# A two-block transformer kernel on one core: forget sums, masks and the permuted modulation sums leave TensorE, and the last weight tile comes by pieces

## The chip, the core and the metric

The kernel runs on one core of a Trainium2 chip. The core has five engines with their own instruction streams: TensorE (PE, with its weight loads PEld), VectorE (DVE), ScalarE (ACT), GpSimd (POOL) and SyncE (SP), whose stream here only issues DMA. They hand work over by semaphores. The metric is the device time of one launch in microseconds, median of the runs.

## The reference

Two transformer blocks over one sequence of 256 tokens with 1024 channels, all in float32.

```python
# first block
mod = c @ w_ada + b_ada                      # shift, scale, gate
h = rmsnorm(x, norm_g) * (1 + scale) + shift
q_a, k_a, v_a, z_a, q_b, k_b, v_b, z_b, f_logit, g_logit = split(h @ w_in)
y_a = stick_breaking(q_a, k_a, v_a)          # w = exp(logsig(z) + sum over later s of logsig(-z)), s < t
y_a = (y_a * silu(z_a)) @ w_o_sb
F = cumsum(log_sigmoid(f_logit + b_forget), axis=1)
y_b = softmax(q_b.k_b / 8 + F[t] - F[s], s <= t) @ v_b      # forgetting attention, 8 heads
y_b = (y_b * silu(z_b)) @ w_o_fox
x = x + gate * ((sigmoid(g0) * y_a + sigmoid(g1) * y_b) @ w_out);  x = rmsnorm(x, final_g)
# second block
mod2 = silu(c_2) @ w_ada_2 + b_ada_2         # sh1, sc1, g1, sh2, sc2, g2
x = x + g1 * (mix(attention(h), conv(h)) @ w_out_2)
h2 = rms_norm(x, norm2_w) * (1 + sc2) + sh2
x = x + g2 * moe(h2)                         # 64 experts, top 1 of 8 groups, top 2 in it; w1, w3, w2
```

## The kernel before, in words

Every engine has one stream written out by hand; nothing is scheduled by a tool. 256 tokens are two tiles of 128 partitions, 1024 channels are eight chunks.

**Up to 290 us: the first block.** The weights come in chunks of 2 MB through a ring of four slots (`RING`, 16 KB per partition each). `proj(q)` is the number of the chunk with 512 columns of w_in, `mod2(q)` that of 512 columns of w_ada_2; they alternate, projection first. `read_by` says for each chunk who must have read it before its slot is filled again; SP issues them in order (L396 to L399). PE works through "units": half a chunk each, 16 matmuls of 256 columns (L618) or 8 of 512 (L629). A float32 matmul shows as two records in the trace. Unit u writes PSUM bank u % 2 and may start when unit u-2 has been taken out (`unit_free`). Chunks 0 to 11 are k, q, v, z of the stick-breaking attention (units 0 to 7), the same of the forgetting attention (8 to 15) and the gate logits (16 to 23). Between the halves of the units the stream places other work: in units 6 to 13 the stick-breaking attention of four head pairs m (`stick_scores`, `stick_after`, `stick_pv`), in units 14 to 22 the forgetting ("fox") attention (`fox_scores`, `fox_transposes`, `fox_pv`), after every odd unit from 5 `mod2_out`.

**mod2.** DVE multiplies a chunk of w_ada_2 by silu(c_2) per partition and adds its eight parts up (`mod2_part`, L1677 and L1679, one half of it per unit). `mod2_out` sums over the partitions on PE; for q = 6 to 9 it takes every eighth column, 8 matmuls, so that the result is laid out as the expert weights are (L653). All these small results go through bank 7, one after another (`misc_done`, `misc_free`).

**Masks and sums on PE.** `stick_after` adds the suffix sums to the scores in PSUM by three matmuls and then adds -1e30 above the diagonal by two more, identity times `never` (L693, L694). `fox_scores` adds -F[s] by three matmuls per head over tiles U that POOL makes from log f (L743 to L745 and L2249 to L2251). DVE's `row_max` then adds the mask, writes the row to SBUF and takes its maximum; ACT takes Exp, DVE the reciprocal, ACT scales, PE transposes.

**silu(z).** ACT writes exp(-z) of units 6, 7, 14, 15; DVE adds 1, takes the reciprocal (3.35 us for 512 columns) and multiplies by z, still in PSUM (L1737), which frees the bank. The gates of units 16 to 21 get the same sigmoid at u = 16 to 21 (`sigmoid_tail`).

**290 to 500 us: the second block's attention and router**, paced by PE again. POOL multiplies the router weights by the second block's scale (L2271 to L2275, after `ab2_ok`).

**From 500 us: the experts.** 16 rounds of four experts; w1, w3 and w2 of four experts are 8 MB each. SP fills eight slots in turn. In the last round w2 comes by quarters, j = 0 to 3, 16 DMAs of 512 KB. After the last quarter PE finishes both halves of the columns (L1167), DVE scales (L2151), PE combines (L1177), DVE adds (L2157), SP stores four pieces (L485).

**The start.** PE multiplies c by w_ada (L549) as four slices of 1 MB land, transposes x (L534), turns the sums into columns (L559) and starts the first halves of units 0 and 1 (L586). `keep_clock(n, bank)` (L525) issues n matmuls of 256 columns whose result nobody reads.

## Time and profile before

| | |
|---|---|
| median of 3 runs | 1414.81 us (1414.81 to 1416.65) |
| span of the profiled execution | 1409.6 us; its own time isn't listed apart from the runs', the median lies 5.2 us over the span |
| PE busy | 1013.6 us, 72% of the span |
| DVE, ACT, POOL busy | 454.7, 167.5, 59.2 us |
| moved by DMA | 503.77 MB, mean 357 GB/s |
| PE busy, 59.0 to 172.0 us | 111.91 of 113.00 us |
| DMA, 518.5 to 1397.7 us | 426 GB/s |
| chain that ended last | PE 50%, DMA 41%, DVE 3%, SP's issues 3% |

The page shows two programs one behind the other. Until about 500 us PE's digits are 9 and the DMA's 4 to 7; after it the DMA's are 9 throughout and PE's 3 to 6. Shares over the whole span say little on either. Two engines' records can overlap, and a matmul's end is modelled: where matmuls follow each other, the distance of two starts is the step, and the printed duration is up to 0.16 us more.

### The profile page before, as it was taken

To read this page: it belongs to the slowest core of one execution; us is meant where nothing else is said; L and a number is where in the kernel's file an instruction comes from. 1 tells how busy PE (TensorE), PEld (TensorE's weight loads), DVE (VectorE), ACT (ScalarE), POOL (GpSimd) and SP (SyncE) were. 2 spreads that over 40 slices of the span, in tenths; PEclk is the share of its full clock that TensorE was granted. 3 is DMA by queue.
4 is the path that set the end of the run, shared out by engine and by line. 5 is a ranking of instruction groups with operands and counts; after the bars stand their busy time and mean duration, and the time that the engine had idled before them with its cause. 6 is when DMAs were issued, how large, how long until landed. Compare 5 with 4: busy or idle time off the path is not lost.

```text
span 1409.6 us, 14940 instructions
## 1 busy us (share of the span) xinstructions
PE 1013.6 (72%) x6025; PEld 530.5 (38%) x6025; DVE 454.7 (32%) x932; ACT 167.5 (12%) x413; POOL 59.2 (4%) x94
## 2 busy tenths in 40 slices
PE   6999999999899985646656366563665646666366
PEld 4677688655456532212222122221222212122121
DVE  1465575542577542112121121211212112121121
ACT  1233232012333200000000000000000000000000
POOL 3101120011020000000000000000000000000000
PEclk9999999999999998868888787897878868788688
DMA  9976655675527899999999999999999999999996
GB/s 357 355 287 238 235 184 213 239 147 192 210 97 294 332 370 428 429 428 428 427 428 429 428 429 428 428 430 427 429 427 429 429 427 430 427 429 427 429 426 271
DMA packets 81551, 503.77 MB, mean 357 GB/s; under 512 B 5670, under 2 KB 11070, under 8 KB 57444
## 3 DMA queue, kind: packets, MB, share of 16 engines
q1 hardware_dynamic: 78784, 496.22, 86.3%
q0 software_dynamic: 2656, 6.93, 2.1%
q8 instruction: 30, 0.49, 0.1%
q14 instruction: 13, 0.11, 0.0%
q10 hardware_dynamic: 68, 0.02, 0.0%
HBM read 501.54 MB, written 1.61 MB: 357 GB/s over the span
## 4 chain that ended last, share of the span: by engine, by line
PE 50%; DMA 41%; DVE 3%; SPq 3%; issue 1%; ACT 0%; DVEq 0%
DMA arena<-in_w_dram 25%; DMA flex<-in_w_dram 15%; PE ps L629 9%; PE ps L618 9%; PE ps L1139 9%; PE ps L1167 7%; PE ps L586 2%; PE ps L1112 2%; PE ps L1184 2%; SPq L408 2%; SPq L415 1%; DMA ring<-in_w_in_dram 1%; DMA arena<-in_w_ada_first_dram 1%; SPq L451 1%; PE ps L865 1%
## 5 line engine op out<-in xcount | busy, mean ns | idle before, releaser
L1139 PE MATMUL ps<-ring,arena 128*32 128x512 f32 x1024 | 259.9, 666 | 102.3 <-DMA arena<-in_w_dram 100.0
L1139 PE MATMUL ps<-arena 128*32 128x512 f32 x768 | 259.5, 667 | 89.9 <-DMA flex<-in_w_dram 88.9
L1167 PE MATMUL ps<-arena 128*32 128x512 f32 x370 | 139.5, 725 | 65.2 <-DMA flex<-in_w_dram 64.5
L1167 PE MATMUL ps<-ring,arena 128*32 128x512 f32 x496 | 138.7, 721 | 60.8 <-DMA arena<-in_w_dram 60.8
L629 PE MATMUL ps<-ring,flex 128*128 128x512 f32 (+1 forms) x336 | 141.3, 576 | 0.6 <-DMA ring<-in_w_in_dram 0.6
L1139 PEld LDWEIGHTS ps<-ring,arena 128*32 128x32 f32 x1024 | 67.2, 121 | 182.4 <-issue 177.8
L1139 PE MATMUL ps<-flex,arena 128*32 128x512 f32 x256 | 128.7, 661 | 0.0
L1139 PEld LDWEIGHTS ps<-arena 128*32 128x32 f32 x768 | 60.4, 121 | 168.8 <-issue 164.6
L618 PE MATMUL ps<-flex,ring 128*128 128x256 f32 x512 | 115.8, 381 | 0.7 <-DVE arena L1737 0.7
L618 PEld LDWEIGHTS ps<-flex,ring 128*128 128x128 f32 x512 | 95.5, 190 | 15.1 <-issue 3.0
L2166 DVE TENSOR_TENSOR arena<-ps,grow 128x1024 f32<-128x1024 f32 x15 | 18.4, 1225 | 256.7 <-PE ps L1167 256.7
L2128 DVE TENSOR_TENSOR arena<-arena,ps 128x512 f32<-128x512 f32 x16 | 11.0, 688 | 243.3 <-PE ps L1139 243.3
L629 PEld LDWEIGHTS ps<-ring,flex 128*128 128x128 f32 x336 | 62.8, 190 | 68.9 <-issue 66.5
L1167 PEld LDWEIGHTS ps<-ring,arena 128*32 128x32 f32 x496 | 33.9, 130 | 105.5 <-issue 105.5
L1167 PEld LDWEIGHTS ps<-arena 128*32 128x32 f32 x370 | 31.3, 130 | 110.2 <-issue 108.7
L1112 PE MATMUL ps<-U,xn 128*128 128x128 f32 x512 | 61.6, 278 | 15.4 <-DVE x_sb L2171 14.9
L1524 ACT ACTIVATE arena<-ps,ab 128x128 f32<-128x128 f32 x64 | 25.8, 454 | 391.9 <-PE ps L1112 391.9
L1184 PE MATMUL ps<-arena,U 128*128 128x512 f32 x120 | 55.5, 605 | 20.2 <-DVE arena L2166 20.2
L1167 PE MATMUL ps<-flex,arena 128*32 128x512 f32 x128 | 69.9, 707 | 0.0
L1112 PEld LDWEIGHTS ps<-U,xn 128*128 128x128 f32 x512 | 58.4, 192 | 28.9 <-issue 25.7
L2123 DVE RECIPROCAL arena<-arena 128x512 f32<-128x512 f32 x16 | 53.6, 3353 | 0.5
L1530 ACT COPY arena<-ps 128x512 f32<-128x512 f32 x16 | 9.4, 586 | 348.1 <-PE ps L1148 348.1
(408 smaller groups left out, 1139.0 us busy)
## 6 DMA issues: line engine op xcount, KB each, us to landing
ring<-in_w_dram SPq DMA_DIRECT2D x90, 2048.0 KB, 19.8
arena<-in_w_dram SPq DMA_DIRECT2D x68, 2048.0 KB, 24.2
flex<-in_w_dram SPq DMA_DIRECT2D x22, 2048.0 KB, 28.8
ring<-in_w_in_dram SPq DMA_DIRECT2D x15, 2048.0 KB, 10.3
ring<-in_w_ada_dram SPq DMA_DIRECT2D x14, 2048.0 KB, 8.9
ring<-in_w_dram SPq DMA_DIRECT2D x20, 512.0 KB, 12.7
arena<-in_w_ada_first_dram SPq DMA_DIRECT2D x8, 1024.0 KB, 14.9
ring<-in_w_out_dram SPq DMA_DIRECT2D x4, 2048.0 KB, 8.9
```

The costliest lines, as they stand in the source:

```text
L408: sp.dma_start(mslot(q), src).then_inc(mring_in[q], 16)
L415: sp.dma_start(mslot(q)[:, o:o + D], src).then_inc(signal if j < 3 else mring_in[q], 16)
L586: mm = pe.matmul(ps[:, FIRST_BANKS[u], m2 * 256:(m2 + 1) * 256], cview(n)[:, c, o:o + P], hT3[:, c, :], start=c == 0 and m2 == 0, stop=c = ...
L618: mm = pe.matmul(ps[:, b, m2 * 256:(m2 + 1) * 256], cview(n)[:, c, (2 * half + m2) * P:(2 * half + m2 + 1) * P], moving[:, c, :], start=c ...
L629: mm = pe.matmul(ps[:, b, 0:n], lhs3[:, c, i * P:(i + 1) * P], rhs[:, c, :], start=c == 0, stop=c == kc_ - 1, skip_group_check=True)
L1112: mm = pe.matmul(ps[:, 4 + c // 2, (c % 2) * P:(c % 2 + 1) * P], xn3[:, i, c * P:(c + 1) * P], sel3[:, i, :], start=i == 0, stop=i == 1)
L1139: mm = pe.matmul(ps[32 * e:32 * e + 32, g, :], xe3[:, c, 32 * e:32 * e + 32], mslot(slots[e])[:, c * W5:(c + 1) * W5], start=c == 0, stop= ...
L1167: mm = pe.matmul(ps[32 * e:32 * e + 32, 2 + n, :], actT3[:, j, 32 * e:32 * e + 32], w, start=j == 0, stop=j == 3, skip_group_check=True)
L1184: mm = pe.matmul(ps[:, (7, 6, 4, 5)[c], :], wc3[:, i, :], ye[:, n * W5:(n + 1) * W5], start=True, stop=True)
L1524: ins = act.activation(xe3[:, c, :], ps[:, 4 + 2 * h, (c % 2) * P:(c % 2 + 1) * P], ACT.Identity, scale=ab[:, 32 + c:33 + c], bias=ab[:, 4 ...
L2123: link_(dve.reciprocal(hE, hE))
L2166: dve.tensor_tensor(ye, ps[:, 2:4, :].rearrange("p a b -> p (a b)"), grow[:, 2 * D:3 * D], ALU.mult).then_inc(m_ye, 1)
```

## The change

**On PE.** `stick_after` loses its two mask matmuls; its first is now that of the late block. `fox_scores` loses the six that add the sums. `mod2_out` for q = 6 to 9 is one matmul with a single column of ones. New are `forget_sums`, two matmuls after `mod2_out` of unit 7 that make -F for all heads at once, and `keep_clock(5)`, `(1)` and `(2)` in the start.

**On DVE.** `stick_never` adds the mask in PSUM (two instructions per pair, before the next `stick_split`), and ACT's `stick_weight` waits for each of them. `row_max` takes a bias from U that holds sum and mask. z is read from SBUF (`Zt`), one unit later than before for each half: z of unit 6 at u = 7, of 7 at 9, of 14 at 15, of 15 at 17. The gates' sigmoids move from u = 16 to 21 to 19 (one), 21 (two), 22 (two), 23 (one). The last two results of the second block's modulation are made after `to_hT` of the second half.

**On ACT.** A copy of z from PSUM to SBUF right after its exp(-z), four in all; it frees the bank.

**On POOL and its DMA queue.** -F goes through DRAM and comes back in all partitions (1 MB); U is that plus the mask, two additions per head. The sums for q = 6 to 9 go to DRAM as a row and come back permuted.

**On SP.** The chunks' order starts with both first projections, so that the third goes into the fourth slot without a wait; `mod2(q)` now stands behind `proj(q + 1)`. The last w2 comes by 28 DMAs: 8 of 512 KB, 12 of 256 KB (2 KB per partition), 8 of 128 KB (1 KB per partition), and `last_outputs` works it off in three ranges of columns, 0:512, 512:768, 768:1024. The stores follow the same ranges.

```diff
-    chunks += [colchunk(w_in, proj_cols[q])] + ([colchunk(ada2, q * W5)] if q < MODQ else [])
+    chunks += [colchunk(w_in, proj_cols[q])] + ([colchunk(ada2, (q - 1) * W5)] if 1 <= q <= MODQ else [])
...
-    return PROJ0 + 2 * q if q < MODQ else PROJ0 + MODQ + q
+    return PROJ0 + (0 if q == 0 else 2 * q - 1 if q <= MODQ else MODQ + q)
...
-    return PROJ0 + 2 * q + 1 if q < MODQ else CONV + 1 + 2 * (q - MODQ)
+    return PROJ0 + 2 * q + 2 if q < MODQ else CONV + 1 + 2 * (q - MODQ)
...
-    for n in [mod2(0), proj(2), mod2(1)] + list(range(RING + 1, NCH)):
+    for n in [proj(2), mod2(0)] + list(range(RING, NCH)):
...
-                for j in range(4):
+                for j in range(2):
                     for e in range(ITEMS):
-                        load_quarter(1, e, ex[ITEMS + e], j, last_in[j] if j < 3 else None)
+                        load_quarter(1, e, ex[ITEMS + e], j, last_in[j])
+                for j, c0, c1, signal in ((2, 0, W5, last_in[2]), (3, 0, W5, last_in[2]), (2, W5, D, half_in),
+                                          (3, W5, W5 + 256, piece_in), (3, W5 + 256, D, None)):
+                    for e in range(ITEMS):
+                        load_columns(e, ex[ITEMS + e], j, c0, c1, signal)
...
-    for m in range(4):
-        n, i = m // 2, m % 2
+    for m, (i, c0, c1) in enumerate(((slice(0, TI), 0, W5), (slice(0, TI), W5, W5 + 256),
+                                     (slice(0, 1), W5 + 256, D), (slice(1, TI), W5 + 256, D))):
...
+    keep_clock(5, 0)
     for k in range(4):
         first_modulation(0, k)
         if k in (1, 2):
             to_features(xn3, k - 1, k)
+    keep_clock(1, 0)
     first_columns(0)
+    keep_clock(2, 0)
...
+    def forget_sums():
+
+        misc_bank()
+        pe.wait_ge(ld_cst, 16)
+        pe.wait_ge(f_lf, 1)
+        le, one = cc(C_LE), C_ONE - C_LE
+        sums = bass.AP(tensor=le.tensor, offset=le.offset, ap=[le.ap[0], [one, 2], [1, P]])
+        pe.matmul(ps[0:8, 7, 0:2 * P], fl[:, 48:56], sums, start=True, stop=False, skip_group_check=True)
+        pe.matmul(ps[0:8, 7, P:2 * P], fl[:, 56:64], le, start=False, stop=True,
+                  skip_group_check=True).then_inc(misc_done, 1)
...
-            lo = 64 * (q % 2)
-            for c in range(DC):
-                mm = pe.matmul(ps[lo:lo + 64, 7, c:c + 1], part[:, c::DC], cst[:, C_ONE:C_ONE + 1],
-                               start=True, stop=True)
+            mm = pe.matmul(ps[0:1, 7, :], cst[:, C_ONE:C_ONE + 1], part[:], start=True, stop=True)
...
-        never = cc(C_NS)
-        never2 = bass.AP(tensor=never.tensor, offset=never.offset, ap=[never.ap[0], [0, 2], [1, P]])
+        pe.matmul(Z_late, cc(C_GE), late(PT), stop=True, **kw)
         pe.matmul(Z_early, cc(C_GE), early(PT), stop=False, **kw)
-        pe.matmul(Z_late, cc(C_GE), late(PT), stop=False, **kw)
-        pe.matmul(Z_early[:, :, P:256], cc(C_ONE), late(PT), stop=True, **kw)
-        pe.matmul(Z_early[:, :, 0:P], IDN, never2, stop=True, **kw)
-        pe.matmul(Z_late, IDN, never2, stop=True, **kw).then_inc(st_c, 1)
+        pe.matmul(Z_early[:, :, P:256], cc(C_ONE), late(PT), stop=True, **kw).then_inc(st_c, 1)
...
-            pe.matmul(ps[:, 2 + b, P:384], q[:, P:T], k[:, 0:T], start=False, stop=False, **kw)
-        for b in range(2):
-            pe.wait_ge(fx_u, 2 * m + b + 1)
-            u = zb(U, b)
-            twice = bass.AP(tensor=u.tensor, offset=u.offset, ap=[u.ap[0], [0, 2], [1, P]])
-            pe.matmul(ps[:, 2 + b, 0:256], cc(C_ONE), twice, start=False, stop=True, **kw)
-            pe.matmul(ps[:, 2 + b, 256:384], cc(C_ONE), u[:, P:256], start=False, stop=False, **kw)
-            pe.matmul(ps[:, 2 + b, 256:384], cc(C_ONE), u[:, 256:384], start=False, stop=True, **kw).then_inc(fx_z, 1)
+            pe.matmul(ps[:, 2 + b, P:384], q[:, P:T], k[:, 0:T], start=False, stop=True, **kw).then_inc(fx_z, 1)
...
+        if u == 7:
+            forget_sums()
...
+    def last_outputs(it, slots, fill, k):
+
+        def part(j, c0, c1, bank):
+            for e in range(ITEMS):
+                mm = pe.matmul(ps[32 * e:32 * e + 32, bank, 0:c1 - c0],
+                               actT3[:, j, 32 * e:32 * e + 32], mslot(slots[e])[:, j * D + c0:j * D + c1],
+                               start=j == 0, stop=j == 3, skip_group_check=True)
+            return mm
+
+        def combine(c0, c1, banks):
+            for i in range(TI):
+                mm = pe.matmul(ps[:, banks[i], 0:c1 - c0], wc3[:, i, :], ye[:, c0:c1], start=True, stop=True)
+                if i == 1 or c1 == D:
+                    mm.then_inc(m_cb, 1)
+
+        c2 = W5 + 256
+        for j in range(2):
+            pe.wait_ge(last_in[j], 16 * ITEMS)
+            part(j, 0, W5, 2)
+            part(j, W5, c2, 3)
+            part(j, c2, D, 0)
+        pe.wait_ge(last_in[2], 2 * 16 * ITEMS)
+        part(2, 0, W5, 2)
+        part(3, 0, W5, 2).then_inc(t_y, 1)
+        pe.wait_ge(half_in, 16 * ITEMS)
+        part(2, W5, c2, 3)
+        part(2, c2, D, 0)
+        pe.wait_ge(t_ye, 1)
+        combine(0, W5, (7, 6))
+        pe.wait_ge(piece_in, 16 * ITEMS)
+        part(3, W5, c2, 3).then_inc(t_y, 1)
+        for q in slots:
+            pe.wait_ge(mring_in[q], landed(k, fill))
+        part(3, c2, D, 0).then_inc(mring_free, 1)
+        pe.wait_ge(t_ye, 2)
+        combine(W5, c2, (4, 5))
+        pe.wait_ge(m_ye, it + 1)
+        combine(c2, D, (1, 2))
+        pe.wait_ge(m_cbf, it + 1)
...
-        act.wait_ge(st_c, m + 1)
+        act.wait_ge(st_cm, 2 * m + 1)
         if m:
             act.wait_ge(st_pv, m)
-        act.activation(early(Pb), Z_early, ACT.Exp)
-        act.activation(late(Pb), Z_late, ACT.Exp).then_inc(st_w, 1)
+        act.activation(late(Pb), Z_late, ACT.Exp)
+        act.wait_ge(st_cm, 2 * m + 2)
+        act.activation(early(Pb), Z_early, ACT.Exp).then_inc(st_w, 1)
...
+                if u == 14:
+                    act.wait_ge(ya_ok, 2)
+                act.copy(Zt[:, (u % 2) * W5:(u % 2 + 1) * W5], ps[:, u % 2, :]).then_inc(unit_free[u % 2], 1)
...
+    def stick_never(m):
+
+        never = cc(C_NS)
+        never2 = bass.AP(tensor=never.tensor, offset=never.offset, ap=[never.ap[0], [0, 2], [1, P]])
+        dve.wait_ge(st_c, m + 1)
+        for z in (Z_late, Z_early[:, :, 0:P]):
+            dve.tensor_tensor(z, z, never2, ALU.add).then_inc(st_cm, 1)
...
-                lo, o = 64 * (k % 2), DC * ((k - 6) // 2)
                 dve.wait_ge(misc_done, misc[0] + 1)
-                dve.tensor_tensor(mod2c[lo:lo + 64, 24 + o:32 + o], ps[lo:lo + 64, 7, 0:DC],
-                                  pcol[lo:lo + 64, o:o + DC], ALU.add).then_inc(misc_free, 1)
+                dve.tensor_copy(mrow[:, (k - 6) * W5:(k - 5) * W5], ps[0:1, 7, :]).then_inc(misc_free, 1)
...
+        if u == 7:
+            dve.wait_ge(misc_done, misc[0] + 1)
+            dve.tensor_copy(F8, ps[0:8, 7, 0:2 * P]).then_inc(misc_free, 1)
+            misc[0] += 1
+        if u in (6, 8, 10, 12):
+            stick_never(u // 2 - 3)
...
-                row_max(u - 14 + b, b, cst[:, C_NM + P:C_NM + 256], cst[:, C_NM:C_NM + 256])
+                dve.wait_ge(fx_u, u - 13 + b)
+                row_max(u - 14 + b, b, zb(U, b)[:, 0:P], zb(U, b)[:, P:384])
...
-        if u in (6, 7, 14, 15):
-            s = sz3[q // 4][:, u % 2, :]
-            dve.wait_ge(e_sig, (u - 5) if u < 8 else (u - 11))
+        if u in (7, 9, 15, 17):
+            z = {7: 6, 9: 7, 15: 14, 17: 15}[u]
+            s = sz3[z // 8][:, z % 2, :]
+            dve.wait_ge(e_sig, (z - 5) if z < 8 else (z - 11))
             sigmoid_tail(s)
-            dve.tensor_tensor(s, s, ps[:, u % 2, :], ALU.mult).then_inc(unit_free[u % 2], 1)
+            dve.wait_ge(unit_free[z % 2], z // 2 + 1)
+            link(dve.tensor_tensor(s, s, Zt[:, (z % 2) * W5:(z % 2 + 1) * W5], ALU.mult))
...
-        if 16 <= u < 22:
-            dve.wait_ge(unit_free[u % 2], u // 2 + 1)
-            sigmoid_tail(gate(u - 16))
+        for g in {19: (16,), 21: (17, 18), 22: (19, 20), 23: (21,)}.get(u, ()):
+            dve.wait_ge(unit_free[g % 2], g // 2 + 1)
+            sigmoid_tail(gate(g - 16))
...
+    dve.wait_ge(ld_pool, LD_MOD2)
+    link(dve.tensor_tensor(mod2c[:, 24:40], mod2c[:, 24:40], pcol[:, 0:16], ALU.add))
+    dve.tensor_copy(ab[:, 40:48], mod2c[:, 24:32])
+    dve.scalar_tensor_tensor(ab[:, 32:40], mod2c[:, 32:40], 1.0, pcol[:, 16:24], ALU.add,
+                             ALU.mult).then_inc(ab2_ok, 1)
...
+            scaled(0, c1, 2, t_y, 1, t_ye)
+            added(0, 0, c1, 7, 1)
+            link_(added(1, 0, c1, 6, 1))
+            scaled(c1, c2, 3, t_y, 2, t_ye)
+            scaled(c2, D, 0, mring_free, it * GROUPS + 3, m_ye)
+            added(0, c1, c2, 4, 2)
+            link_(added(1, c1, c2, 5, 2))
+            link_(added(0, c2, D, 1, 3))
+            added(1, c2, D, 2, 4).then_inc(m_cbf, 1)
...
+        if m == 1:
+            pool.wait_ge(misc_free, 4)
+            pool.dma_start(f_dram, F8).then_inc(st_pool, 16)
+        elif m == 2:
+            pool.wait_ge(st_pool, ST_GATES)
+            pool.dma_start(FB, bass.AP(tensor=f_dram.tensor, offset=f_dram.offset,
+                                       ap=[[0, P], [1, H * 2 * P]])).then_inc(ld_pool, 16)
...
-            pool.wait_ge(fx_z, h - 1)
-        u = zb(U, h % 2)
-        pool.tensor_scalar(u[:, 0:P], cc(C_LE), fl[:, 48 + h:49 + h], None, ALU.mult)
-        pool.tensor_scalar(u[:, P:256], cc(C_ONE), fl[:, 48 + h:49 + h], None, ALU.mult)
-        pool.tensor_scalar(u[:, 256:384], cc(C_LE), fl[:, 56 + h:57 + h], None, ALU.mult).then_inc(fx_u, 1)
-    pool.wait_ge(misc_free, 17)
+            pool.wait_ge(fx_m, h - 1)
+        u, f = zb(U, h % 2), FB[:, h * 2 * P:(h + 1) * 2 * P]
+        pool.tensor_tensor(u[:, 0:P], f[:, 0:P], cst[:, C_NM + P:C_NM + 2 * P], ALU.add)
+        pool.tensor_tensor(u[:, P:384], f, cst[:, C_NM:C_NM + 2 * P], ALU.add).then_inc(fx_u, 1)
+    pool.wait_ge(misc_free, 12)
+    pool.dma_start(m_dram, mrow).then_inc(st_pool, 16)
+    pool.wait_ge(st_pool, ST_MOD2)
+    pool.dma_start(mod2c[:, 24:40].rearrange("p (v c) -> p v c", v=2),
+                   m_dram.rearrange("o (v p c) -> p (o v) c", v=2, p=P)).then_inc(ld_pool, 16)
```

PE's stream in units 7 and 8, before: the matmuls between two halves of a unit are those of the stick-breaking attention.

```order
L618 MATMUL ps<-flex,ring 128x256 x8
L657 MATMUL ps<-cst,modt 128x1 x4
L618 MATMUL ps<-flex,ring 128x256 x8
L690 MATMUL ps<-flex,cst 128x512
L691 MATMUL ps<-flex,cst 128x256
L692 MATMUL ps<-flex,cst 128x2x128
L693 MATMUL ps<-cst 128x2x128
L694 MATMUL ps<-cst 128x256
L618 MATMUL ps<-flex,ring 128x256 x8
L675 MATMUL ps<-arena 128x256
```

And now, in the same place:

```order
L642 MATMUL ps<-flex,ring 128x256 x8
L689 MATMUL ps<-cst,modt 128x1 x4
L674 MATMUL ps<-cst,fl 8x256
L675 MATMUL ps<-cst,fl 8x128
L642 MATMUL ps<-flex,ring 128x256 x8
L720 MATMUL ps<-flex,cst 128x256
L721 MATMUL ps<-flex,cst 128x512
L722 MATMUL ps<-flex,cst 128x2x128
L642 MATMUL ps<-flex,ring 128x256 x8
L707 MATMUL ps<-arena 128x256
```

Two matmuls have gone from between the halves of unit 8, and the two of `forget_sums` stand in front of it.

DVE's stream from u = 6 to u = 8, before; L1633 and L1634 are the start of `stick_split`, L1642 is `stick_log`.

```order
L1636 TENSOR_SCALAR U<-ps 128x2x128
L1625 TENSOR_SCALAR arena<-arena 128x512
L1626 RECIPROCAL arena<-arena 128x512
L1737 TENSOR_TENSOR arena<-arena,ps 128x512
L1679 SCALAR_TENSOR_TENSOR mod2p<-ring,colB,mod2p 128x512 x4
L1642 SCALAR_TENSOR_TENSOR flex<-flex,U 128x768
L1721 TENSOR_TENSOR mod2c<-ps,colB 128x4
L1625 TENSOR_SCALAR arena<-arena 128x512
L1626 RECIPROCAL arena<-arena 128x512
L1737 TENSOR_TENSOR arena<-arena,ps 128x512
L1677 TENSOR_SCALAR modt<-ring,colB 128x512
L1679 SCALAR_TENSOR_TENSOR modt<-ring,colB,modt 128x512 x3
```

And now; L1701 is `stick_log`, L1709 is `stick_never`.

```order
L1746 SCALAR_TENSOR_TENSOR mod2p<-ring,colB,mod2p 128x512 x4
L1701 SCALAR_TENSOR_TENSOR flex<-flex,U 128x768
L1786 TENSOR_TENSOR mod2c<-ps,colB 128x4
L1791 COPY xn<-ps 8x256
L1684 TENSOR_SCALAR arena<-arena 128x512
L1685 RECIPROCAL arena<-arena 128x512
L1811 TENSOR_TENSOR arena<-arena,xn 128x512
L1744 TENSOR_SCALAR modt<-ring,colB 128x512
L1746 SCALAR_TENSOR_TENSOR modt<-ring,colB,modt 128x512 x3
L1709 TENSOR_TENSOR ps<-ps,cst 128x256
L1709 TENSOR_TENSOR ps<-ps,cst 128x2x128
L1692 TENSOR_SCALAR flex<-ps 128x2x256
```

Of the two sigmoids one is left here, behind the copy of the forget sums; the mask's two additions stand behind it and the half `mod2_part`.

DVE's stream at the end of the projections, before; the L1716 is that of the last `mod2_out`, L1751 makes yT of the fox heads, L1659 takes the first gate row out of bank 7.

```order
L1716 TENSOR_TENSOR mod2c<-ps,pcol 64x8
L1751 TENSOR_TENSOR arena<-arena,ps 128x512 x2
L1761 COPY ab<-mod2c 128x8
L1762 SCALAR_TENSOR_TENSOR ab<-mod2c,colB 128x8
L1761 COPY ab<-mod2c 128x8
L1762 SCALAR_TENSOR_TENSOR ab<-mod2c,pcol 128x8
L1763 COPY rt<-ab 128x1
L1659 COPY modt<-ps 128x512
```

And now, with L1782, L1825 and L1726 in their places:

```order
L1782 COPY spare<-ps 1x512
L1825 TENSOR_TENSOR arena<-arena,ps 128x512 x2
L1684 TENSOR_SCALAR arena<-arena 128x512
L1685 RECIPROCAL arena<-arena 128x512
L1834 COPY ab<-mod2c 128x8
L1835 SCALAR_TENSOR_TENSOR ab<-mod2c,colB 128x8
L1836 COPY rt<-ab 128x1
L1726 COPY modt<-ps 128x512
```

A sigmoid (L1684, L1685) stands before the copy of the gate row, which PE waits for.

## Rows read from the trace of the kernel before

**Rows 1.** Windows: us, busy (x) of PE, PEld, DVE, ACT, POOL, clock, DMA, GB/s.
```profile
21.00:22.00 1.00, 1.00 (x3) 0.78 (x3) 0.00 (x0) 0.05 (x1) 1.00 (x3) 0.50 1.05 424
59.00:172.00 113.00, 111.91 (x487) 78.94 (x486) 63.88 (x102) 34.42 (x53) 15.86 (x27) 1.00 0.73 262
172.00:250.40 78.40, 78.12 (x433) 66.37 (x433) 50.00 (x80) 20.14 (x59) 8.83 (x12) 1.00 0.56 202
518.50:1397.70 879.20, 514.16 (x3603) 199.77 (x3594) 175.78 (x238) 41.97 (x90) 0.00 (x0) 0.81 1.00 426
```

**Rows 2.** Waits of PE from 50 to 287 us: total, times, longest.
```profile
PE ps L618 <- DVE arena L1737: 0.7, 1, 0.7
```

**Rows 3.** Timeline of PE, 20 to 29 us: start, us, operation, idle before.
```profile
20.10 8.83 PE L586 MATMUL ps<-flex,ring 128*128 128x256 f32 x32 [1.06 <-ACT flex L1247]
```

**Rows 4.** Line L549 on PE: ns of one, min/median/max.
```profile
L549 PE MATMUL ps<-arena,c x128: 379/379/636, 9.3 to 38.0; 128*32 128x256 f32 x128
```

**Rows 5.** Timeline of PE, 80 to 106 us.
```profile
80.60 0.59 PE L693 MATMUL ps<-cst 128*128 128x256 f32 x2
81.03 0.59 PE L694 MATMUL ps<-cst 128*128 128x256 f32 x2
...
101.37 3.62 PE L618 MATMUL ps<-flex,ring 128*128 128x256 f32 x16
104.92 0.48 PE L675 MATMUL ps<-arena 64*128 64x256 f32 x1
```

**Rows 6.** Timeline of DVE, 88 to 105 us.
```profile
88.63 0.43 DVE L1625 TENSOR_SCALAR arena<-arena 128x512 f32<-128x512 f32 x1
...
93.08 3.11 DVE L1679 SCALAR_TENSOR_TENSOR mod2p<-ring,colB,mod2p 128x512 f32<-128x512 f32 x4
...
101.61 0.48 DVE L1677 TENSOR_SCALAR modt<-ring,colB 128x512 f32<-128x512 f32 x1
102.13 2.33 DVE L1679 SCALAR_TENSOR_TENSOR modt<-ring,colB,modt 128x512 f32<-128x512 f32 x3
```

**Rows 7.** Timeline of PE, 152 to 192 us.
```profile
152.47 1.02 PE L649 MATMUL ps<-mod2p,cst 128*128 128x512 f32 x2
...
161.18 0.70 PE L743 MATMUL ps<-U,cst 128*128 128x256 f32 x2
...
163.04 7.07 PE L618 MATMUL ps<-flex,ring 128*128 128x256 f32 x32
...
189.92 2.08 PE L653 MATMUL ps<-cst,mod2p 128*64 128x1 f32 x16
```

**Rows 8.** Timeline of POOL, DVE and ACT, 164 to 188 us.
```profile
164.05 3.11 DVE L1679 SCALAR_TENSOR_TENSOR mod2p<-ring,colB,mod2p 128x512 f32<-128x512 f32 x4
...
164.17 1.10 POOL L2249 TENSOR_SCALAR U<-cst,fl 128x128 f32<-128x128 f32 x1
...
182.33 0.29 DVE L1650 CUSTOM_DVE_ANT_0 flex<-ps,cst 128x128 f32<-128x128 f32 x1 [2.68 <-PE ps L745]
...
187.26 0.40 ACT L1321 ACTIVATE Pb<-Pb,soft 128x128 f32<-128x128 f32 x1 [2.10 <-DVE soft L1732]
```

**Rows 9.** Timeline of PE, 250 to 257 us.
```profile
250.45 1.92 PE L521 MATMUL ps<-ring,c 128*32 128x512 f32 x16 [0.33 <-DVE mod2c L1716]
...
255.86 1.02 PE L809 MATMUL ps<-modt,cst 128*128 128x512 f32 x2
```

**Rows 10.** Chain that ended last, 1355 to 1410 us: start, us, what.
```profile
1364.65 0.33 SPq L415
...
1382.04 15.67 DMA flex<-in_w_dram
...
1399.77 3.66 PE ps L1177 x8
...
1403.52 0.69 DVE x_sb L2157
```

**Rows 11.** Timeline of SP's DMA issues, 453 to 466 us.
```profile
453.44 11.69 SPq L422 DMA_DIRECT2D spare<-in_w_dram  x6
```

103 lines of the change are left out of this document (53 added, 50 removed).

## The prediction, made blind

> **What bounds the kernel now.** I read the windows first, since the page's sums mix two programs. Between 59 and 172 us PE is busy 111.91 of 113.00 us and the DMA 0.73; between 172 and 250.4 us PE 78.12 of 78.40, the DMA 0.56. From 518.5 to 1397.7 us the DMA is at 1.00 and 426 GB/s while PE works 514.16 of 879.20 us [rows 1]. So until about 500 us each microsecond that PE saves moves what follows, and after it only bytes count. Are the two linked? The expert weights can start only when PE has worked off what lies in the slots before, so the 879 us begin earlier by what PE saves, at the same length. PE's savings inside the expert stage are worth nothing. Then I read PE's waits, to see what a shorter unit uncovers: from 50 to 287 us only one wait for DVE's z appears, 0.7 us [rows 2]. Everything else in those 200 us is PE's own work.
>
> The sum is made in times of the profiled execution (span 1409.6 us); the median of the runs lies 5.2 us above it, and I take the difference off the median, 1414.81 us. A difference of 0.2% (2.8 us) is about what a measurement of this kernel can tell from none.
>
> **The start.** 32 half-unit matmuls take 8.83 us from 20.10 [rows 3], with the clock granted at 0.50 in the window at 21 [rows 1]; the same 32 take 7.07 us later [rows 7]. So the low clock costs 1.76 us behind PE's idle 1.06 us. In the first slices the longest L549 took 636 ns against 379 [rows 4], again the low clock. The change puts matmuls into three gaps. Five of 0.86 us (twice 0.43, the step of 256 columns [rows 5]) are 4.3 us, which begin in idle time before the first slice at 9.3 us [rows 4] and delay its first matmuls a little; the one and the two before and behind `first_columns` fill the gap of 1.06 us. Bounds: +1.1 us (they delay and the clock stays) and -1.8 us. I take -1.5, near the low end, since the slow stretch follows directly on the idle.
>
> **Masks off PE.** L693 starts at 80.60, L694 at 81.03: a step of 0.43 us for a float32 matmul of 256 columns [rows 5]. Two steps times four pairs: -3.4 us.
>
> **Forget matmuls.** From L743's start at 161.18 to the next unit at 163.04 are 1.86 us [rows 7]. Four pairs: -7.4 us.
>
> **Permuted sums.** 16 records of L653 take 2.08 us, the one matmul of 512 columns 1.02 us (L649) [rows 7]. Four times -1.06: -4.2 us.
>
> **z out of PSUM at once.** The wait of 0.7 us [rows 2] goes. ACT's copies (four of 0.6 us; 128 columns take 0.40 [rows 8]) lie in a queue that has nothing else between two units of 7 us. These four terms: -15.7 us.
>
> **What `forget_sums` adds.** 256 and 128 columns, 0.43 + 0.22 = 0.65 us. It needs bank 7 again, which DVE's small addition of `mod2_out` has to free; PE waits here as it does for the same hand-over before L521, 0.33 us [rows 9]. I take 0.45: +1.1 us.
>
> **What `stick_never` adds.** This is the new chain: PE's sums, DVE's two additions, ACT's two Exp, PE's `stick_scores` of the next pair. Its wait stands in DVE's queue behind the sigmoid and half a `mod2_part`. For pair 1: unit 8's second half starts at 101.37 and ends at 104.92 [rows 5], so a half is 3.55 us; `stick_after` before it was six steps (2.58), now four (1.72). Counting back, the unit's first half began at 95.24; now, 0.86 less and 1.1 more, at about 95.5. PE then wants the chain's result at 95.5 + 3.55 + 1.72 + 3.55 = 104.3. DVE begins its sigmoid behind the copy of the forget sums at about 96.05; it and the product take 4.45 (from 88.63 to 93.08), the half `mod2_part` 2.85 (from 101.61 to 102.13 + 2.33) [rows 6]. DVE is free at 103.35. An addition of 256 columns in PSUM isn't in the trace. The nearest rows: 0.29 us for 128 columns with a maximum [rows 8] and 0.69 for 512 (L2157) [rows 10]; I take 0.4 each. The second is done at 104.15, the last Exp some 0.6 later, PE goes on at 104.95: +0.65 us. Pair 2 has no forget copy but a unit earlier sigmoid product in front: +0.35. Pairs 0 and 3 have no sigmoid in front: 0. Together +1.0; with 0.2 and 0.69 per addition, from 0.3 to 2.5.
>
> **The last bank-7 results.** The row of `mod2(9)` is now copied as 512 columns of one partition, 0.69 as L2157 [rows 10] instead of about 0.17, and L521 waits for it: +0.55. Behind it stand yT (1.28 us), gate 21's sigmoid (4.45 less the product, 3.8 [rows 6]), two small copies (0.35) and the copy of the gate row, without which L809 can't start. From L521's start to L809's were 5.41 us without a wait [rows 9]. DVE reaches the gate row 0.69 + 1.28 + 3.8 + 0.35 = 6.1 us after the bank's matmul, has it at 6.8, PE sees it at 7.0; it wants it at 6.25. PE waits 0.75. Together +1.3 us (bounds 0.5 and 4, if other work holds the sigmoid up).
>
> **At no cost.** The third projection ahead: PE had no wait for a landing between 50 and 287 us [rows 2], so it only keeps the 1.5 us of the start from being lost to a late chunk; without that cover the term of the start is 0. `mod2(q)` behind `proj(q + 1)`: DMA at 0.73 [rows 1] leaves it some 6 us. POOL's additions for a head, at most 3 x 1.10 us, and 6.6 for a pair, stand against a pair's 17 us; the trip of -F through DRAM has 35 us, that of the permuted row over 70 us before the router asks. DVE's load in units 21 and 22 is 0.69 + 4 x 3.83 = 16.0 us against PE's 16.5: it just fits; if not, PE waits 1 or 2 us.
>
> **The tail.** SP's issues run ahead and the last transfer ends at 1382.04 + 15.67 = 1397.71 us; the chain then takes until 1403.52 + 0.69 = 1404.21 [rows 10]: 6.5 us. The bytes are the same, so the landing keeps its place. What stays behind it is a quarter of 256 columns, its scaling, two combines of 256 and additions of 0.41 for 0.69. Combining columns 0:512, and much of 512:768, is done before. I count 4.5 us: -2.0, with bounds -0.5 (last pieces land together) and -3.5.
>
> A rule that bears on the pieces: the Trainium skill, "DMA: Bandwidth & Descriptors", section "Specifications", gives 512 B as the least transfer at line rate. By it pieces of 1 KB per partition lose nothing and the term stays -2.0; no row here has such pieces at a full queue, so the trace can't confirm it.
>
> **Sum.** -15.7 + 1.1 + 1.0 + 1.3 - 1.5 - 2.0 = -15.8 us. 1414.81 - 15.8 = **1399.0 us**.
>
> **Rivals.**
>
> *A, the fox chain becomes the bound.* Its maximum is at 182.33 and the scaling at 187.26, done 0.9 later [rows 8]: 5.8 us, against a unit of 7.07 [rows 7] with 0.86 beside it. 2.1 us of slack. POOL now adds tiles out of SBUF while DVE is in this chain. If DVE stood still while POOL did (6.6 us per pair), 4.5 us per pair would be left over; for three pairs +13.5, and the time 1412.5. Against it: DVE's L1679 took 3.11 us at 164.05, beside POOL's L2249 [rows 8], and 3.11 at 93.08 alone [rows 6]; POOL's instruction was the long one. But POOL read less there than it will. Chance 0.06.
>
> The rule beside it is the Trainium skill's, "SBUF — State Buffer", section "Who interferes with whom": a DVE instruction with two SBUF inputs and a GpSimd one that reads SBUF exclude each other, whoever is first holds the port. By it the sum would be rival A's, 1412.5. The equal 3.11 us speak against a full block of DVE, and for POOL waiting.
>
> *B, nothing is passed on.* If the experts' start hung on the stream of bytes before it, PE's gain would be gone at 518 us and only the tail's 2.0 left: 1412.8. Against it: the DMA is at 0.56 [rows 1] while PE is full. Chance 0.06.
>
> *C, the new waits are larger.* If each of the four `stick_never` costs 2 us instead of 0.25 on average, +7: 1406. It needs the additions at 0.69 and something more in front, such as a late `stick_log`. Chance 0.05.
>
> *D, slower than before: the pieces are bound by SP.* Six issues took 11.69 us at SP, 1.95 each [rows 11]. If that were the price of an issue, 28 of them from 1364.65 [rows 10] would take 54.6 us, until 1419.3; the landing would come some 1.2 us after, 22.7 late. -15.8 + 22.7 = +6.9: 1421.7. The issues bind from 33.06 / 28 = 1.18 us each, and the kernel is slower than before from about 1.70. Against it: the DMA was at 1.00 all through [rows 1], so SP stood at a full queue and the 1.95 us are the queue's pace, not SP's. Chance 0.03.
>
> **How the numbers follow.** The forecast has 0.80. Its own range: the bounds of the additions (-0.7, +1.5), the start (-0.3, +2.6), the bank (-0.8, +2.7), the tail (-1.5, +1.5), taken together, not all at one end: 1396 to 1403. Widened towards A, B and C, and a little down for POOL and PE gains that I count at nothing, 1394.5 to 1406. Faster by over 0.2%: main, C, and half of A and B at their softer ends, less a little for what I don't see: 0.88. Within 0.2%: 0.09. Slower: 0.03.
>
> **What would show it.** In the profile after: a unit pair of the fox stage (two units of 7.07 with what lies between) 1.9 + 1.1 us shorter; PE's waits with one on ACT's early Exp (under 1 us, twice), one before the forget sums (0.3 to 0.5), one before the gate row (about 0.75), none on z; the clock at 1.00 between 20 and 24 us; the experts' start 13 to 14 us earlier and their length the same to 1 us; from the last landing to the end 4.5 us. Wrong if: PE waits on DVE for over 2 us in units 14 to 22 (A), the gain by 500 us is under 8 us (B, C), or DMA's share falls under 1.00 in the last 30 us (D).

## The result and the profile after

The changed kernel takes 1398.13 us (median of 4 runs, 1397.66 to 1399.18); the kernel before 1414.81 (1410.11 to 1416.65). The ratio is 0.9892, 95% interval 0.9873 to 0.9911, that is -15.3 us (-12.6 to -18.0). A second comparison on another chip gave 0.9893 (0.9878 to 0.9908). Forecast were 1399.0 us and -15.8.

The two profiled executions differ by less, 1409.6 - 1397.4 = 12.2 us. In every run listed the time is the span plus 1.7 to 1.8 us, so the profiled execution of before stands for a time of about 1411.4. The executions of the kernel before lie between 1408.9 and 1416.7 us, those of the changed kernel between 1396.4 and 1399.2. These two traces therefore explain 12.2 us part by part; the other 3 are the spread of the kernel before. A second trace of it (before_again, below) holds 2.7 us of such a spread, in the experts' stretch.

| stretch ends with | before | after | difference |
|---|---|---|---|
| first projection unit over all of K (L629, L653) | 59.08 | 58.00 | -1.1 |
| first gate row (L521, L542) | 250.45 | 236.22 | -14.2 |
| the second block's first unit | 287.25 | 273.69 | -13.6 |
| the unit behind the wait for w_in | 354.85 | 342.67 | -12.2 |
| start of the experts' full stream (SP) | 523.71 | 511.56 | -12.2 |
| last addition ends | 1404.21 | 1392.20 | -12.0 |

At the third line -13.8 us were expected. Then 1.4 us are lost in one wait, and the tail (the work around and behind the last landing, the moment when the last weights have arrived) gives nothing in this pair. The windows of the changed kernel (us, busy of PE, PEld, DVE, ACT, POOL, clock, DMA, GB/s), which answer to [rows 1]:

```profile
21.00:22.00 1.00, 1.00 (x6) 0.90 (x5) 0.25 (x1) 0.39 (x2) 1.00 (x3) 1.00 1.07 428
59.00:172.00 113.00, 111.64 (x484) 78.55 (x483) 71.12 (x115) 36.76 (x58) 13.21 (x25) 1.00 0.74 266
172.00:236.00 64.00, 63.38 (x317) 49.16 (x315) 49.67 (x77) 19.62 (x58) 6.34 (x8) 1.00 0.66 237
507.00:1385.00 878.00, 513.35 (x3622) 199.71 (x3618) 176.51 (x239) 41.98 (x90) 0.00 (x0) 0.81 1.01 427
```

The clock at 21 us is 1.00 (2.4 GHz) instead of 0.50 (1.2 GHz), PE is as full as before, DVE took over 7 us of work between 59 and 172 us, and the experts' stretch is as long as it was.

The waits of PE between 50 and 274 us (total, times, longest), for [rows 2]:

```profile
PE ps L542 <- DVE spare L1782: 0.8, 1, 0.8
...
PE ps L707 <- ACT Pb L1348: 0.7, 2, 0.4
PE ps L832 <- DVE modt L1726: 0.4, 1, 0.4
PE ps L674 <- DVE mod2c L1786: 0.3, 1, 0.3
```

The wait for z is gone, and the four new ones are those that were foreseen, where they were foreseen. PE's timeline at the start, in the stick-breaking stage and in the fox stage (start, us, operation, idle before), for [rows 3, 5, 7, 9]:

```profile
20.44 7.14 PE L607 MATMUL ps<-flex,ring 128*128 128x256 f32 x32
...
93.68 0.60 PE L674 MATMUL ps<-cst,fl 128*8 128x256 f32 x2 [0.25 <-DVE mod2c L1786]
...
103.76 0.48 PE L707 MATMUL ps<-arena 64*128 64x256 f32 x1 [0.44 <-ACT Pb L1348]
...
123.15 0.48 PE L707 MATMUL ps<-arena 64*128 64x256 f32 x1 [0.28 <-ACT Pb L1348]
...
158.11 0.60 PE L766 MATMUL ps<-arena 64*128 64x256 f32 x4
158.64 7.17 PE L642 MATMUL ps<-flex,ring 128*128 128x256 f32 x32
...
182.93 1.02 PE L686 MATMUL ps<-mod2p,cst 128*1 128x512 f32 x2
...
236.22 1.92 PE L542 MATMUL ps<-ring,c 128*32 128x512 f32 x16 [0.84 <-DVE spare L1782]
...
242.20 1.12 PE L832 MATMUL ps<-modt,cst 128*128 128x512 f32 x2 [0.40 <-DVE modt L1726]
```

The 32 matmuls of the start take 7.14 us (8.83 before). The first unit of a fox pair stands directly behind the scores, and `mod2_out` is one matmul of 1.02 us. DVE's masks in PSUM, and POOL beside DVE in the fox stage (same columns):

```profile
102.31 0.76 DVE L1709 TENSOR_TENSOR ps<-ps,cst 128x256 f32<-128x256 f32 x2
```

```profile
131.63 0.45 POOL L2340 TENSOR_TENSOR U<-arena,cst 128x128 f32<-128x128 f32 x1
132.05 0.71 POOL L2341 TENSOR_TENSOR U<-arena,cst 128x256 f32<-128x256 f32 x1
...
161.92 1.17 POOL L2341 TENSOR_TENSOR U<-arena,cst 128x256 f32<-128x256 f32 x1
```

```profile
159.57 0.17 DVE L1721 TENSOR_SCALAR soft<-soft 128x2 f32<-128x2 f32 x1
...
160.37 0.62 DVE L1721 TENSOR_SCALAR soft<-soft 128x2 f32<-128x2 f32 x1
160.91 3.52 DVE L1746 SCALAR_TENSOR_TENSOR mod2p<-ring,colB,mod2p 128x512 f32<-128x512 f32 x4
```

The two masks cost 0.76 us together (0.8 taken). POOL's addition takes 0.71 us alone and 1.17 beside L1746; DVE's L1721 0.17 alone and 0.62 beside POOL, and four L1746 3.52 instead of 3.11 [rows 8].

The unit behind the wait for w_in, in the trace of before, then in that of after:

```profile
354.85 7.13 PE L629 MATMUL ps<-ring,flex 128*128 128x512 f32 x16 [0.58 <-DMA ring<-in_w_in_dram]
...
365.26 8.79 PE L865 MATMUL ps<-ring,arena 128*32 128x256 f32 x64
```

```profile
342.67 8.83 PE L653 MATMUL ps<-ring,flex 128*128 128x512 f32 x16 [1.96 <-DMA ring<-in_w_in_dram]
...
354.78 7.10 PE L888 MATMUL ps<-ring,arena 128*32 128x256 f32 x64
```

The wait has grown from 0.58 to 1.96 us, and the unit behind it takes 8.83 instead of 7.13: the granted clock is 0.50 there. Before, this 1.7 us fell on another line (8.79 against 7.10), so in this pair of profiles they cancel.

### The profile page after: what moved, and what is told of

The parts are those of the page before. It is cut to its first block, busy times and chain, and to the rows that moved or that the text cites. A ratio compares the mean times of both kernels' runs of the same rounds, so it can differ in the third digit from the quotient of the medians.

```text
span 1397.4 us, 14850 instructions
## 1 busy us (share of the span) xinstructions
PE 1002.2 (72%) x5961; PEld 516.5 (37%) x5961; DVE 464.3 (33%) x945; ACT 169.4 (12%) x417; POOL 55.1 (4%) x90
## 4 chain that ended last, share of the span: by engine, by line
PE 48%; DMA 41%; DVE 5%; SPq 4%; issue 1%; ACT 1%; DVEq 0%; ACTq 0%
DMA flex<-in_w_dram 20%; DMA arena<-in_w_dram 19%; PE ps L653 10%; PE ps L1202 9%; PE ps L642 9%; PE ps L1233 7%; PE ps L1175 2%; PE ps L1239 2%; SPq L419 2%; DMA arena<-in_w_ada_first_dram 2%; SPq L432 1%; PE ps L607 1%; DVE arena L1685 1%; SPq L401 1%; DMA ring<-in_w_in_dram 1%
## 5 line engine op out<-in xcount | busy, mean ns | idle before, releaser
L1202 PE MATMUL ps<-ring,arena 128*32 128x512 f32 x1024 | 257.2, 660 | 99.9 <-DMA arena<-in_w_dram 98.5
L1202 PE MATMUL ps<-arena 128*32 128x512 f32 x768 | 256.8, 661 | 89.6 <-DMA flex<-in_w_dram 86.4
L1233 PE MATMUL ps<-arena 128*32 128x512 f32 x354 | 134.3, 738 | 63.5 <-DMA flex<-in_w_dram 63.5
L1233 PE MATMUL ps<-ring,arena 128*32 128x512 f32 x464 | 133.4, 739 | 62.2 <-DMA arena<-in_w_dram 62.2
L653 PE MATMUL ps<-ring,flex 128*128 128x512 f32 (+1 forms) x336 | 143.0, 582 | 2.0 <-DMA ring<-in_w_in_dram 2.0
L1202 PE MATMUL ps<-flex,arena 128*32 128x512 f32 x256 | 127.3, 655 | 0.0
L653 PEld LDWEIGHTS ps<-ring,flex 128*128 128x128 f32 x336 | 63.4, 192 | 71.4 <-issue 67.6
L1233 PE MATMUL ps<-flex,arena 128*32 128x512 f32 x112 | 64.4, 740 | 0.0
## 6 DMA issues: line engine op xcount, KB each, us to landing
arena<-in_w_ada_first_dram SPq DMA_DIRECT2D x8, 1024.0 KB, 15.3
```

The source lines that it names most:

```text
L653: mm = pe.matmul(ps[:, b, 0:n], lhs3[:, c, i * P:(i + 1) * P], rhs[:, c, :], start=c == 0, stop=c == kc_ - 1, skip_group_check=True)
L1202: mm = pe.matmul(ps[32 * e:32 * e + 32, g, :], xe3[:, c, 32 * e:32 * e + 32], mslot(slots[e])[:, c * W5:(c + 1) * W5], start=c == 0, stop= ...
L1233: mm = pe.matmul(ps[32 * e:32 * e + 32, 2 + n, :], actT3[:, j, 32 * e:32 * e + 32], w, start=j == 0, stop=j == 3, skip_group_check=True)
```

## The experiments

Times are medians; each was compared with runs of the kernel before on the same chip. The ratios' intervals are about 0.0015 to 0.002 to either side (2 to 3 us), the spread of before for the most part; the changed kernels among themselves repeat better, so they are compared with each other.

| run | us | ratio to before | PE at the second block's first unit | instruction packet | w_in wait | experts' stream starts | from there to the last addition |
|---|---|---|---|---|---|---|---|
| before_again | 1413.84 | 1.0007 | 287.14 | 317, 365 | 0.67 | 522.48 | 883.2 |
| after_again | 1398.06 | 0.9893 | 273.43 | 333 | 1.56 | 510.86 | 880.3 |
| whole_tail | 1398.86 | 0.9906 | 273.57 | 333 | 1.78 | 511.26 | 881.0 |
| no_keep_clock | 1397.04 | 0.9889 | 274.61 | 304, 344 | 0.68 | 509.48 | 880.8 |
| short_pad | 1399.21 | 0.9903 | 274.70 | 334 | 1.65 | 512.24 | 879.8 |
| keep_pad | 1395.68 | 0.9882 | 273.87 | 324 | 0.58 | 508.64 | 880.5 |
| masks_on_pe | 1397.92 | 0.9895 | 277.05 | 328 | 0.61 | 513.60 | 880.7 |
| sigmoids_later | 1394.22 | 0.9873 | 272.36 | 322 | 0.55 | 507.10 | 879.4 |
| fox_filled | 1404.63 | 0.9944 | 283.20 | 321 | 0.43 | 517.83 | 879.8 |
| order_before | 1403.70 | 0.9940 | 276.71 | 336 | 1.84 | 517.53 | 879.2 |
| fine_pieces | 1401.86 | 0.9931 | 274.21 | 334 | 1.56 | 509.98 | 883.2 |
| later_and_short | 1394.03 | 0.9869 | 273.07 | 323 | 0.38 | 509.34 | 877.7 |

The column "instruction packet" is the microsecond in which a packet of the queue q8 (kind "instruction") shows near the wait. "w_in wait" is PE's wait for the chunk of w_in near 342 us (354 in the kernel before). The columns behind the ratio are of the one profiled execution; the first pair's last two values are 523.71 and 880.5 before, 511.56 and 880.6 after.

**after_again, before_again.** The same two kernels once more.

> The changed kernel, unaltered, against the kernel before on another chip run. The account: PE reaches the second block's first unit 13.6 us earlier in any execution. What differs from execution to execution is the wait for the projection weights near 342 us (1.96 us in the profile shown, 0.58 in that of before). Theory (the wait is chance): the ratio is 0.989 to 0.9905 (-13.5 to -15.5 us), and the wait near 342 us is again between 0.5 and 2 us. Rival (the new order of the chunks causes the wait): it is about 2 us in every profile of the changed kernel.

> The kernel before against itself: ratio 1.000 within its interval (some 0.1%). Its profile gives a second reading of the wait for the projection weights near 354 us. Chance: anywhere from 0.5 to 2 us. Rival: again 0.6 us.

Measured: 0.9893 and 1.0007. The wait is 1.56 us in the changed kernel and 0.67 in that before. Two profiles of each don't decide between chance and cause; whole_tail has 1.78 us, a third on the side of cause. The clock loss at 365 us of the first profile of before did not come back in the second. That one has another, behind the last landing: after an idle time of 4.18 us the clock falls to 0.50 at 1398.8 us, and the eight combining matmuls take 4.64 us instead of 3.66 [rows 10].

```profile
1397.65 2.58 PE ps L1167 x16
1400.22 4.64 PE ps L1177 x8
```

From the last landing to the last addition it is 8.1 us there, 6.5 in the first profile of before and in whole_tail, and 3.7 to 5.1 in the eleven profiles with pieces, none of which has the clock at 0.50 in that stretch. That the pieces spare the kernel this loss is not shown: of the three profiles with quarters one has it.

**whole_tail.** The last w2 by quarters.

```
-                        for j in range(2):
+                        for j in range(4):
                             for e in range(ITEMS):
-                                load_quarter(1, e, ex[ITEMS + e], j, last_in[j])
-                        for j, c0, c1, signal in (...): load_columns(...)
+                                load_quarter(1, e, ex[ITEMS + e], j, last_in[j] if j < 3 else None)
```

> The changed kernel with the last w2 by quarters and the last outputs as before (16 DMAs of 512 KB). As the prediction has it: 2.0 us slower than the changed kernel (bounds 0.5 and 3.5). By the profile of the changed kernel: 0, since the pieces land together and later relative to the stream's start (875.2 us against 874.0), which eats the 1.1 us that the work behind the last landing is shorter.

Measured: 0.8 us slower. From the stream's start to the last addition it takes 1392.27 - 511.26 = 881.0 us, the changed kernel 880.6 and 880.3. So the pieces are worth 0.4 to 0.8 us here, not 2.0, which is hardly more than the executions differ: this kernel's are three of 1398.0 to 1398.9 and two of 1400.4 and 1401.1. Whether these two have the clock loss of before_again no trace shows.

**no_keep_clock.** Without the eight idle matmuls.

```
-            keep_clock(5, 0)
...
-            keep_clock(1, 0)
             first_columns(0)
-            keep_clock(2, 0)
```

> The changed kernel without the eight idle matmuls of the start. As predicted: 1.5 us slower. By the profile (PE begins its first whole projection unit at 58.00 instead of 59.08): 1.1 us slower. In its profile the clock is granted at 0.50 between 21 and 24 us. Rival (the new chunk order and not the clock gave the 1.1 us): 0, and PE begins at 58.0 again.

Measured: 1.0 us *faster*, though PE is 0.9 us later at the second block. Both expectations fail on the total; the clock (0.50 from 20.4 us) and PE's later start are as expected. The wait of the w_in chunk is 0.68 us and the unit behind it 7.13: the idle matmuls gain 0.9 us at the start and lose 1.3 + 1.7 near 342. Between the two kernels nothing differs there but the count of instructions ahead and the start. The DMA queues of the changed kernel from 332 to 333 us, and of no_keep_clock from 344 to 345 (packets, MB, share of 16 engines):

```profile
q1 hardware_dynamic: 363, 0.37, 108.8%
q8 instruction: 1, 0.02, 7.3%
```

```profile
q1 hardware_dynamic: 189, 0.39, 105.2%
q8 instruction: 1, 0.02, 7.0%
```

7.3% of 16 engines for 1 us are 1.17 us on one engine. In the changed kernel the packet falls between the issue of the two transfers (327.47 and 331.25) and the landing of the second (342.67); without the idle matmuls it comes when that has landed (342.31). From issue to PE's start are 11.42 us with it and 10.15 without. That gives the fetch theory: one DMA engine carries the instructions first, and a transfer over all engines lands with the last of them.

**short_pad, keep_pad.** The count of instructions alone, in PE's idle time before 6.7 us:

```
             pe.wait_ge(ld_id, 16)
+            for _ in range(8):          # short_pad, on no_keep_clock; 10 in keep_pad, on the changed kernel
+                pe.matmul(ps[0:1, 0, 0:1], cst[:, C_ID:C_ID + 1], cst[:, C_ID:C_ID + 1], start=True, stop=True)
             pe.wait_ge(ld_rowsA, 48)
```

> The changed kernel without its eight idle matmuls, but with eight of one column in their place, put into PE's idle time before the first rows land, so that PE's stream has as many instructions as the changed kernel's and its clock in the start is as without them. Fetch theory: a packet of PE's instructions (queue q8, one packet of 16 KB) comes at 332 to 335 us again, among the two transfers that precede the wait of L653; the wait is 1.5 to 2 us, the clock falls to 0.50 behind it, and the time is 1399 to 1400 us, some 2.8 slower than without the eight (1397.04). Rival (the wait comes because PE is 1.1 us earlier from the start): packet or not, the wait is 0.7 us and the time 1397 us.

> The changed kernel with ten more matmuls of one column in PE's idle time before the first rows land. Eight instructions moved the packet from 344 to 332.5 us, so ten more put it at about 319, before the transfers are issued (327.5 and 331.3 us). Fetch theory: the wait of L653 is 0.6 to 0.7 us, the clock stays at 1.00 behind it, the start keeps its 1.1 us: 1398.06 - 1.1 - 1.7 = 1395.3 us. Rival (earliness): the wait stays 1.6 to 2 us and the time 1398 us.

Measured: 1399.21 and 1395.68, both on the fetch theory's side, 2.2 us slower and 2.4 us faster than the kernels they were made from. The start of the experts' stream, which leaves out what comes behind it, says it more clearly: 512.24 - 509.48 = 2.8 us later and 511.56 - 508.64 = 2.9 us earlier. The packet of keep_pad came at 324 us and not at the expected 319. PE at that unit in short_pad, then in keep_pad:

```profile
343.37 8.83 PE L652 MATMUL ps<-ring,flex 128*128 128x512 f32 x16 [1.65 <-DMA ring<-in_w_in_dram]
```

```profile
341.48 7.13 PE L655 MATMUL ps<-ring,flex 128*128 128x512 f32 x16 [0.58 <-DMA ring<-in_w_in_dram]
```

Earliness is out: keep_pad is early and doesn't wait, short_pad is late and does. In the 14 profiles the packet lies between issue and landing where the wait is 1.56 us or more (six), and elsewhere where it is 0.68 or less (eight, the first profile of before among them). That the delayed engine is the one with the packet is an inference from the 1.17 us; no row gives the packets by engine.

**masks_on_pe.** The two mask matmuls back, DVE's additions out.

```
-                pe.matmul(Z_early[:, :, P:256], cc(C_ONE), late(PT), stop=True, **kw).then_inc(st_c, 1)
+                pe.matmul(Z_early[:, :, P:256], cc(C_ONE), late(PT), stop=True, **kw)
+                pe.matmul(Z_early[:, :, 0:P], IDN, never2, stop=True, **kw)
+                pe.matmul(Z_late, IDN, never2, stop=True, **kw).then_inc(st_c, 1)
...
-                if u in (6, 8, 10, 12):
-                    stick_never(u // 2 - 3)
```

> The changed kernel with the two mask matmuls of each pair back on PE and without DVE's additions. Until unit 24 it should be 3.4 us later and save the two waits for ACT (0.44 and 0.28 measured): 2.7 us later. Its PE stream has eight matmuls more ahead of the wait of L653, so by the fetch theory the packet comes at about 321 us, the wait is 0.7 us and the clock stays: 1398.06 + 2.7 - 2.8 = 1398.0 us. Rival (no part for the fetch): 1398.06 + 2.7 = 1400.8 us.

Measured: 1397.92 us. From the first full unit to the second block PE needs 277.05 - 58.76 = 218.29 us against 273.69 - 58.00 = 215.69: 2.6 us, which is the net worth of moving the masks (2.4 in the prediction: 3.4 - 1.0). Yet the median is that of the changed kernel, as the fetch theory had it (1398.0): its packet comes at 328 us, not at 321, but ahead of the transfers, and the wait is 0.61 us. The trace doesn't bear out the rest. The profiled execution took 1402.58 us and the other four 1397.65 to 1397.99; in it the clock falls after all, behind the next waits:

```profile
355.08 8.79 PE L892 MATMUL ps<-ring,arena 128*32 128x256 f32 x64
```

So its stream starts 2.0 us later than that of the changed kernel, 3.4 less 1.4 of wait, and its end lies another 1.3 us later behind the last addition. Why the other four were faster no trace shows. Judged by the median alone, the moved masks would look like a change without effect.

**sigmoids_later.** On keep_pad:

```
-                if u in (7, 9, 15, 17):          # z 6, 7 now at the end of u = 8, 10, behind stick_log
+                if u in (15, 17):
...
-                for g in {19: (16,), 21: (17, 18), 22: (19, 20), 23: (21,)}.get(u, ()):
+                for g in {19: (16,), 21: (17, 18), 22: (19, 20)}.get(u, ()):
...
+                        if j == 1: sigmoid_tail(gate(5))     # behind mod_row
```

> The kernel of keep_pad with three sigmoids moved on DVE: those of z 6 and 7 behind stick_log of u = 8 and 10, that of gate 21 behind the copy of the gate row and the modulation row. The waits of PE for ACT's Exp (0.44, 0.28) and for the gate row (0.40) go: 1.1 us faster than keep_pad. Rival: the product of u = 9 or the next pair's mask then waits instead (DVE has 14.5 us of work in a pair of 19.4 us), same time or slower.

Measured: 1.5 us faster than keep_pad, 1394.22, and the stream starts 1.5 us earlier. PE's waits for ACT's Exp in this stage and for the gate row are gone from its list of waits, that before the forget sums (0.3) and that for the row of `mod2(9)` (0.8) remain.

**fox_filled.** Eight idle matmuls in each `fox_scores`:

```
+                for _ in range(8):
+                    pe.matmul(ps[:, 2, 384:512], IDN, cst[:, 0:P], start=True, stop=True, skip_group_check=True)
```

> The changed kernel with eight matmuls of 128 columns in each fox_scores, whose result nobody reads: 8 x 0.22 = 1.76 us of PE per pair, 7.0 in all, nearly what the change took out there (7.4). If PE's time before 500 us passes to the end one to one, unit 24 and the experts' stream come 7.0 us later; the 32 instructions also move the instruction packets, so the end is 7.0 us later give or take the 1.1 and 1.7 us at the wait of L653: 1402.3 to 1405.1. Rival B (the stream of bytes before 518 us sets the experts' start): under 2 us later, 1400 or less.

Measured: 1404.63 us, 6.6 slower. The eight cost 2.2 us per pair, not 1.76: from the first full unit to the second block 283.20 - 58.79 = 224.41 us, 8.7 more than the changed kernel. Less 1.5 us of wait and 1.7 of clock that its packet at 321 us doesn't cost, plus 0.8 of a later start (58.5 to 58.9 us in all four kernels run on this chip), this is 6.3; the stream starts 517.83 - 511.56 = 6.3 later. PE's time goes through one to one; rival B is out.

**order_before.** The chunks in the old order.

```
-            chunks += [colchunk(w_in, proj_cols[q])] + ([colchunk(ada2, (q - 1) * W5)] if 1 <= q <= MODQ else [])
+            chunks += [colchunk(w_in, proj_cols[q])] + ([colchunk(ada2, q * W5)] if q < MODQ else [])
...          # and proj, mod2, read_by and the first loads with it
```

> The changed kernel with the chunks in the order of the kernel before (third projection behind the first slice of w_ada_2, mod2(q) ahead of proj(q + 1)). PE's stream is the same, so the packet, the wait of L653 (1.6 to 2 us) and the clock behind it stay: 1398.1 us as the changed kernel. Rival (the order ahead is what lets PE use the gain of the start): a new wait for the projection near 57 to 59 us and 0.5 to 1.1 us slower.

Measured: 5.6 us slower, beyond both. PE has a wait that neither kernel had, at unit 6 and not at 57 us:

```profile
77.24 3.72 PE L642 MATMUL ps<-flex,ring 128*128 128x256 f32 x16 [2.09 <-DMA ring<-in_w_in_dram]
```

The fourth projection is issued at 57.26 us, behind two chunks of w_ada_2, and PE starts on it at 77.24; it wanted it at 75.15. In before_again the same chunk was issued at 57.09 and PE waited 0.2 us, until 75.21: the old order is at its edge. A packet of instructions shows at 62 us here, within the transfer, and at 45 and 73 there, which may be the 2 us between the two; no run separates it. With the wait of w_in the unit takes 10.21 us, 1.4 more than in the changed kernel, at a clock of 0.50 for longer. The stream starts 517.53 - 511.56 = 6.0 us later: 0.8 of the start (the other kernels of this chip have it too), 2.1, 1.4, and 1.7 that I didn't take apart. At 508.8 us the clock is at 0.50 once more for 3.4 us, with PE busy throughout, which would be 1.7. So the wait itself is 2.1 of the 5.6 us; the rest is the chip's start and two losses of clock, and no run shows whether they follow from the order.

**fine_pieces.** All of the last w2 by 256 columns.

```
-                        for j in range(2): ... load_quarter(...)
+                        for j, c0, c1, signal in (
+                                [(j, c, c + 256, last_in[j]) for j in range(2) for c in range(0, D, 256)] + ...
```

> The changed kernel with all of the last w2 in pieces of 128 KB (1 KB per partition), 64 DMAs. Rival D asked for 1.95 us of SP per issue: 64 of them would take 125 us, and the end comes some 90 us later. The profile of the changed kernel shows 1.08 us while SP stands at a full queue and 0.43 while it doesn't: 0.43 x 64 = 27.5 us, less than the 33 us of the stream, no bound by SP. Rows of 1 KB moved at 371 GB/s against 410: for 8.4 MB 22.6 us against 20.5, so 2 us slower than the changed kernel, 1400 us. By the Trainium skill, "DMA: Bandwidth & Descriptors", section "Specifications", rows of 1 KB lose nothing: 1398 us.

Measured: 3.8 us slower than the changed kernel (executions from 1399.83 to 1404.18; the profile is of the fastest). In the trace the experts' stretch is 2.6 to 2.9 us longer, 883.2 against 880.6 and 880.3. SP's issues, and the windows of that kernel (columns as above), then windows of the kernel before with rows of 4 KB:

```profile
1369.46 0.43 SPq L432 DMA_DIRECT2D arena<-in_w_dram  x1
1369.93 0.91 SPq L432 DMA_DIRECT2D ring<-in_w_dram  x2
1370.88 0.43 SPq L432 DMA_DIRECT2D flex<-in_w_dram  x1
```

```profile
1365.00:1370.00 5.00, 5.00 (x36) 1.44 (x32) 0.00 (x0) 0.00 (x0) 0.00 (x0) 0.65 1.08 343
1375.00:1380.00 5.00, 3.65 (x48) 1.46 (x48) 0.00 (x0) 0.23 (x1) 0.00 (x0) 1.00 0.88 283
```

```profile
1380.00:1385.00 5.00, 5.00 (x40) 1.60 (x36) 0.00 (x0) 0.00 (x0) 0.00 (x0) 0.72 1.03 412
1385.00:1390.00 5.00, 3.52 (x35) 1.25 (x28) 0.69 (x1) 0.59 (x1) 0.00 (x0) 1.00 1.02 407
```

SP needs 0.47 us from one DMA to the next (0.43 and a gap), and 128 KB per 0.47 us are 279 GB/s: at this size it does bind, as the 0.88 and 283 GB/s show. My 27.5 us for 64 issues hid that, since the gaps and a stall of 5 us at the full queue come on top: they took 36.5 us. And the rows of 1 KB move 320 GB/s per engine share of 1.00 (343 / 1.08, 283 / 0.88), those of 4 KB 400 (412 / 1.03).

This run also has the packet among the transfers and the wait of 1.56 us, to the hundredth that of after_again, and yet its clock stays at 1.00 behind it. First after_again, then fine_pieces:

```profile
342.01 8.83 PE L653 MATMUL ps<-ring,flex 128*128 128x512 f32 x16 [1.56 <-DMA ring<-in_w_in_dram]
```

```profile
342.80 7.13 PE L653 MATMUL ps<-ring,flex 128*128 128x512 f32 x16 [1.56 <-DMA ring<-in_w_in_dram]
```

So the delayed landing goes with the packet, and the loss of clock only mostly with the delay.

**later_and_short.** `keep_clock(3)` instead of `keep_clock(5)`, twelve instead of ten small ones, on sigmoids_later.

> The kernel of sigmoids_later with three instead of five idle matmuls ahead of the first slice and twelve of one column (the same count of instructions). PE can start the first slice at about 10.5 instead of 12.2 us, but the fourth slice then sets the pace: 0 to 0.3 us faster than sigmoids_later (1394.22), if the clock still is at 1.00 from 20 us. Rival: three are too few, the clock falls at 20 us, 1.5 us slower.

Measured: 1394.03 against 1394.22, the same, and the clock at 20 us stays at 1.00. PE now waits 1.07 us for a projection chunk at 21 us instead. That the totals agree is partly chance: in the traces the stream starts 2.2 us later than in sigmoids_later (the clock is at 0.50 for 3.4 us from 500.6) and the stretch behind it is 1.7 us shorter.

## Why the prediction was right, step by step

**The bound** holds. PE's time before 500 us goes through to the end (fox_filled), and the stretch under DMA is 879.2 to 881.0 us long in eleven of the fourteen profiles, whatever stands in front. The others are before_again and fine_pieces (883.2 both) and later_and_short (877.7).

**The four terms on PE** came as worked out: masks (four PE steps of 0.86), U (1.86 us gone per pair), `mod2_out` (1.06 each), z (0.7). masks_on_pe measures the first apart, 2.6 us net of what it brings with it.

**`forget_sums`**: from `mod2_out` to the next unit 94.43 - 92.48 = 1.95 us against 0.81, +1.14 (1.1 forecast). **`stick_never`**: 0.44 + 0.28 = 0.72 (0.65 + 0.35 forecast), at pairs 1 and 2 only. **The last bank-7 results**: the row of `mod2(9)` +0.5, from L542 to L832 5.98 us against 5.41 [rows 9], +1.1 (1.3 forecast). The order of DVE's queue, read against rows of before, was enough for all three.

**The start**: -1.1 where -1.5 was taken (0.8 to 1.2 between kernels on one chip). The clock's 1.7 us came in full (8.83 to 7.14), but the first five idle matmuls took 4.6 us, as at the low clock (4.3 assumed, 2.15 by their step of 0.43), and the first slice began at 12.25 instead of 9.3, so that PE was 0.3 us later at 20 us.

**The tail** is the term that was mis-sized: -2.0 forecast, 0.4 to 0.8 by whole_tail, at the small end of its bounds (0.5 to 3.5). The step "the bytes are the same, so the landing keeps its place" failed, and what stays behind it was larger. Windows of the changed kernel:

```profile
1380.00:1382.00 2.00, 1.06 (x24) 0.40 (x20) 0.00 (x0) 0.00 (x0) 0.00 (x0) 1.00 1.07 371
1386.00:1387.00 1.00, 1.00 (x4) 0.38 (x2) 0.00 (x0) 0.00 (x0) 0.00 (x0) 1.00 0.05 18
1387.00:1388.00 1.00, 1.00 (x14) 0.36 (x16) 0.42 (x1) 0.00 (x0) 0.00 (x0) 1.00 0.00 0
```

The last landing comes 875.7 us after the stream's start instead of 874.0. The first of these windows, with rows of 1 and 2 KB, moves 371 GB/s at a share of 1.07, so short rows are a likely reason. But the spread is as large: 874.5 in whole_tail and 875.0 in before_again with quarters, 872.7 to 875.8 with the change's pieces. And the pieces meant to come one by one land close to each other, the last three groups at 1384.5, 1385.9 and 1387.2 us; PE then has the combine of columns 0:512 (1.9 us) in front of the last part. PE and DVE in this stretch:

```profile
1384.56 0.40 PE L1132 MATMUL ps<-arena 128*32 128x256 f32 x1 [0.74 <-DMA flex<-in_w_dram]
...
1385.56 1.98 PE L1139 MATMUL ps<-arena,U 128*128 128x512 f32 x4
1387.47 0.40 PE L1132 MATMUL ps<-arena 128*32 128x256 f32 x1
...
1389.38 1.99 PE L1139 MATMUL ps<-arena,U 128*128 128x256 f32 x8 [0.83 <-DVE arena L2228]
1390.54 1.66 DVE L2234 TENSOR_TENSOR x_sb<-x_sb,ps 128x256 f32<-128x256 f32 x4 [0.89 <-PE ps L1139]
```

From the last landing (issued at 1380.29, 6.9 us before) to the last addition (1392.20) are 5.0 us, against 6.5 before and 4.5 forecast: 1.5 gained, and the later landing takes it back in this pair. The Trainium skill, "DMA: Bandwidth & Descriptors", section "Specifications", has line rate from 512 B. The measurement decides otherwise here: 320 GB/s per share of 1.00 in rows of 1 KB, 400 in rows of 4 KB.

**"At no cost", the order of the chunks**: right in the sum, wrong in its worth. I wrote that the third projection only keeps the gain of the start, and that moving `mod2(q)` costs nothing, since PE had no wait for a landing in the trace of before. That a load comes in time doesn't say by how much: order_before waits 2.1 us at unit 6, and is 5.6 slower in all with what came on top. With the new order no profile has such a wait.

**What no step had** is the packet of instructions among the transfers before 342 us: 1.4 us of wait, and 1.7 more, since the clock fell behind it. Adding and removing instructions moves it, and the trace of before had the row for it (queue q8), unread.

**Rivals.** A is out by the waits, but its mechanism is there. DVE lost 0.45 + 0.41 us per pair beside POOL, POOL 0.46 on one instruction and more on the others, and the chain's slack of 2.1 us hid it; the 6.6 us of POOL's work per pair that I had bounded were 3.3. By the Trainium skill, "SBUF — State Buffer", section "Who interferes with whom", the two exclude each other in turn, and the trace agrees in direction: each is longer beside the other. B is out by fox_filled. C: the waits came smaller, not larger. D is out: an issue costs SP 0.47 us where the queue isn't full and not 1.95; with the 28 pieces SP doesn't bind (1.18 would be needed on average), with 64 of 128 KB it does.

That 1399.0 lies so near 1398.13 is partly luck. The working is right on PE's terms until 290 us (-13.6 against -13.8). Behind them the sum has 1.2 to 1.6 us too much for the tail and nothing for the 3.1 us at the wait of w_in, of which the profile of before pays 1.7 as well; against these stands a spread of the kernel before, 3 us above its profiled execution, that the sum didn't hold either.

## What to carry to other kernels

Where a kernel is bound by one engine, a term read as "steps of the timeline times count" holds to a few tenths of a microsecond, and so does a new wait, if what stands in the waiting engine's queue is added up. Ask of every transfer that was in time by how much it was: a wait that is missing from the list says nothing of the slack. And compare landmarks along the run before you credit a total to an edit: here eight or ten instructions that do nothing moved the total by 2.2 to 2.4 us and the start of the experts' stream by 2.8 to 2.9, as much as moving the masks did (2.6). The best version run, sigmoids_later with its ten small matmuls (1394.22 us, 0.9873 of before), and later_and_short (1394.03) rest partly on where such a packet falls.

## What the runs showed of the hardware

- A packet of instructions (the page of after has 29 of them with 0.48 MB, some 16 KB each) took 1.17 us of one engine's time. In the six profiles where one fell between issue and landing of the 2 MB transfer, PE could start on it 11.0 to 11.4 us after its issue, in the eight others after 9.8 to 10.2. That the packet holds up an engine which the transfer also needs is the likely reason, not a row. Eight matmuls more in PE's stream moved the packet earlier by 11 to 12 us, ten by 8.5.
- With an idle time of 1.56 to 1.96 us before that unit, behind one of 0.88, the granted clock was 0.50 at the unit's beginning in five of six profiles, and the unit took 8.83 instead of 7.13 us (10.21 once); in the sixth, fine_pieces with 1.56, it stayed at 1.00. With 0.38 to 0.68 us it was 1.00 there in all eight, but in two of them (before, masks_on_pe) it fell some 10 us later, for the same 1.7 us.
- Behind the last landing the clock fell to 0.50 in one of three profiles with the old tail: 8.1 us to the last addition instead of 6.5.
- Where the queue isn't full, a DMA issue takes SP 0.47 us. Rows of 1 KB move 320 GB/s per share of 1.00 and rows of 4 KB 400.
